# One of four channel tiles of a causal depthwise convolution computed on GpSimd

## The chip, the cores and the metric

The kernel runs on one core of a Trainium2 chip. A core has five engines that run their own queues of instructions side by side and meet at semaphores: TensorE (PE, matrix products), VectorE (DVE), ScalarE (ACT), GpSimd (POOL) and SyncE (SP, which here only issues DMAs). The metric is the time on the device of one execution in microseconds (us).

## What is computed

One transformer block (attention beside a gated linear recurrence, then an MLP) is followed by two layers of a second block. Both work on 256 tokens of width 2048 in float32. The change touches the second block alone, in each of whose layers a convolution runs over the tokens of 1024 channels, with a kernel of its own of 31 taps for every channel:

```python
u_val, u_gate = jnp.split(conv_in + glu_b[l], 2, axis=-1)
u = u_val * jax.nn.sigmoid(u_gate)
u = causal_depthwise_conv(u, dw_w[l], dw_b[l])        # 31 taps, groups = channels
u = jax.nn.silu(layer_norm(u, conv_ln_g[l], conv_ln_b[l]))
u = u @ w_pw[l] + b_pw[l]
conv_out = u * jax.nn.silu(conv_gate)
y = jnp.concatenate([mla_out, conv_out], axis=-1) @ w_out[l]
x = x + gate * y
```

## The kernel before

Every large product is made in three matmuls (or two wider ones) from a high and a low part of the weights and of the activations. Weights come by DMA into four buffers RAW0 to RAW3. A chunk is taken in halves: ScalarE copies a half into WH (line 1932), which rounds it, and VectorE subtracts that from RAW and writes the low part WL (line 1087). Such a subtraction is called a split here. There are four WH and four WL buffers (`NHL = 4`); ScalarE may write half j when TensorE has finished half j - 4 (`half_done`), VectorE when ScalarE has written it (`high`), and TensorE may use it when VectorE has split it (`split`). Nearly all of the kernel's time TensorE goes through one such half after another.

All smaller work is written as strands, generators that each engine's program steps once for every half of weights that TensorE takes. So on each engine a strand's piece stands in the queue between two halves, and its place is fixed when the program is built.

The convolution is such a strand. The channels are eight tiles of 128, four to a part. UV holds the gated input (256 tokens behind 30 zeros) and UG the running sum, both 128 x 256 for a tile. ScalarE makes tap 0 of each tile with the bias (line 2152), and VectorE adds taps 1 to 30 in place, one instruction a tap and tile (line 1446): 120 instructions for part 0 (tiles 0 to 3, semaphore `taps0`), 120 for part 1 (tiles 4 to 7, `taps1`). `tap_steps` orders them by tap, then tile, three or four in a step. Part 1 can start only when its gated input has been made, about halfway through. When both are done, `channel_norm` starts on TensorE with a sum over the channels (`n_sum`), ahead of which TensorE waits for `taps0` and `taps1`. GpSimd has nothing to do in this kernel.

Of the kernel before, what the change touches and what calls it, by code (L numbers as in the profile page):

```python
# [12 lines left out]
ALU = mybir.AluOpType  # L13
# [226 lines left out]
def weight_course(t):  # L240
# [105 lines left out]
    "ones_row lb lb_sig r_f r_log r_key r_cum r_last r_att r_diag r_gap r_exp0 r_edge r_cross r_ax "  # L346
    "r_diff r_exp r_pair r_level r_head r_out r_sq r_ss r_ms r_root r_wide r_unit r_done "
    "rope_v rope_t up_low up_sum up_relu up_sq up_h up_l "
    "gc uz taps0 taps1 l_sq l_ss l_rms l_root l_mul l_h l_l "
    "q_rope_sq h_sq h_sum h_rope_sum h_ms h_root h_gain h_rot h_sin h_rope h_wide h_apply "  # L350
    "a_score a_in a_top a_exp a_add a_probs a_tp a_pt a_pv a_out o_h o_l "
    "n_sum n_part n_mean n_sub n_sq n_ss n_ms n_root n_scale n_silu p_h p_l pw g_mm g_col g_out g_row g_mul x2"
# [3 lines left out]
def tiles(nc, ctx):  # L356

    ncol, nconst = columns()[1], constant_places()[1]
    m = {}

    def sb(c, name, shape, dt=F32, align=128):
        m[name] = c.enter_context(nc.sbuf_tensor(name, shape, dt, align_bytes=align))

    sb(ctx, "X", [128, 2, 2048], align=1024)
    sb(ctx, "HT", [128, 16, 2, 256], F32R)
    m["HTh"], m["HTl"] = m["HT"][:, :, 0, :], m["HT"][:, :, 1, :]
    for i in range(NRAW):
        sb(ctx, f"RAW{i}", [128, 2048])
    for i in range(NHL):
        sb(ctx, f"WH{i}", [128, 1024], F32R)  # L370
    for i in range(NHL):
        sb(ctx, f"WL{i}", [128, 1024], F32R)
    sb(ctx, "PK", [128, ncol])
    sb(ctx, "CN", [128, nconst])
    sb(ctx, "Y", [128, 2, 2048], align=1024)
    sb(ctx, "HS", [128, 256])
    with ExitStack() as c:
        for name in ("E1", "LK1"):
            sb(c, name, [128, 1024])
    sb(ctx, "CB", [128, 2048])  # L380
    sb(ctx, "ST", [128, 64])
    sb(ctx, "MODC", [128, 2, 3, 16])
    for i in range(8):
        m[f"PS{i}"] = ctx.enter_context(nc.psum_tensor(f"PS{i}", [128, 512], F32))
    sb(ctx, "VT", [128, 4, 256], align=1024)
    sb(ctx, "MXB", [128, 256])
    with ExitStack() as c:
        sb(c, "FR", [128, 8, 256])
        sb(c, "QR", [128, 8, 256])
        sb(c, "QA", [128, 8, 256])  # L390
        sb(c, "KA", [128, 256])
        sb(c, "VA", [128, 2, 128])
        sb(c, "SINK", [128, 16])
        sb(c, "S", [128, 8, 384])
        sb(c, "MX", [128, 4, 8])
        sb(c, "SM", [128, 2, 8])
        sb(c, "RES", [128, 1024])
        sb(c, "LB", [128, 2, 8])
        for name in ("LQ0", "LQ1"):
            sb(c, name, [128, 512])  # L400
        sb(c, "FC", [128, 16])
        sb(c, "AXX", [128, 2, 4, 128])
        with ExitStack() as d:
            for name in ("KK", "B", "E0", "LK0"):
                sb(d, name, [128, 1024])
        with ExitStack() as d:
            sb(d, "AH", [128, 8, 256], F32R, align=1024)
            sb(d, "AL", [128, 8, 256], F32R, align=1024)
    sb(ctx, "COS", [128, 256])
    sb(ctx, "SIN", [128, 256])  # L410
    with ExitStack() as c:
        sb(c, "GB1", [128, 2048])
        sb(c, "SJ", [128, 512])
    with ExitStack() as c:
        sb(c, "Uh", [128, 32, 256], F32R, align=1024)
        sb(c, "Ul", [128, 32, 256], F32R, align=1024)
    with ExitStack() as c:
        sb(c, "UV", [128, 8, 286])
        sb(c, "UG", [128, 8, 256])
        sb(c, "KV", [128, 3, 256])  # L420
        with ExitStack() as d:
            with ExitStack() as f:
                sb(f, "QN", [128, 8, 256], align=1024)
                sb(f, "QP", [128, 4, 256])
                sb(f, "KN", [128, 8, 256])
                sb(f, "KP", [128, 4, 256])
            with ExitStack() as f:
                sb(f, "GT", [128, 2048], align=1024)
                sb(f, "OH", [128, 8, 256], F32R, align=1024)
                sb(f, "OL", [128, 8, 256], F32R, align=1024)  # L430
            d.enter_context(nc.sbuf_tensor("SPACE", [128, 6144], F32, align_bytes=1024))
            sb(d, "V2", [128, 2, 1024])
            sb(d, "R2", [128, 256])
            with ExitStack() as f:
                sb(f, "KVh", [128, 2, 256], F32R, align=1024)
                sb(f, "KVl", [128, 2, 256], F32R)
                sb(f, "QLh", [128, 4, 256], F32R)
                sb(f, "QLl", [128, 4, 256], F32R)
            with ExitStack() as f:
                sb(f, "SQR", [128, 4, 256], align=1024)  # L440
            with ExitStack() as f:
                sb(f, "S2", [128, 8, 384], align=1024)
                sb(f, "MX2", [128, 2, 8])
                sb(f, "SM2", [128, 2, 8])
    return m


def views(m):

    col, place = columns()[0], constant_places()[0]  # L450

    def pk(name):
        a, n = col[name]
        return m["PK"][:, a:a + n]

    def cn(name):
        a, n = place[name]
        return m["CN"][:, a:a + n]

    return pk, cn  # L460
# [16 lines left out]
def tensor_program(e, m, signals, plan):  # L477
    chunks, group = plan
    pe = Queue(e, signals)
    pk, cn = views(m)  # L480
# [450 lines left out]
    def channel_norm(L, taps):  # L931
        UG, UV = m["UG"], m["UV"]
        while any(strand in course.strands for strand in taps):
            yield
        for n in range(15):
            if n == 0:
                b = small()
                pe.wait_ge("taps0", 124 * L + 124)
                pe.wait_ge("taps1", 124 * L + 124)
                spread_sum(b, lambda i: UG[:, i, :]).then_inc(signals["n_sum"], 1)  # L940
                free[b] = ("n_part", 2 * L + 1)
            if n == 2:
                b = small()
                pe.wait_ge("n_part", 2 * L + 1)
                mm(b, 0, 256, ones, m["R2"][:, :], True, True).then_inc(signals["n_sum"], 1)
                free[b] = ("n_mean", L + 1)
            if n == 6:
                b = small()
                spread_sum(b, lambda i: UV[:, i, 0:256], lambda i: ("n_sq", 4 * L + i // 2 + 1)).then_inc(
                    signals["n_ss"], 1)  # L950
                free[b] = ("n_part", 2 * L + 2)
            if n == 8:
                b = small()
                pe.wait_ge("n_part", 2 * L + 2)
                mm(b, 0, 256, ones, m["MXB"][:, :], True, True).then_inc(signals["n_ss"], 1)
                free[b] = ("n_root", L + 1)
            yield
# [61 lines left out]
    for L in range(2):  # L1019
# [10 lines left out]
        taps = [course.start(convolution(L, 0))]  # L1030
# [40 lines left out]
def vector_program(e, m, signals, plan):  # L1071
    chunks, group = plan
    dve = Queue(e, signals)
    pk, cn = views(m)
# [52 lines left out]
    def scaled(t, *cs):  # L1127
        for c in cs:
            e.tensor_scalar(Y[:, t, 512 * c:512 * c + 512], X[:, t, 512 * c:512 * c + 512], ST[:, 54 + t:55 + t], None,  # L1129
                            ALU.mult).then_inc(signals["xs"], 1)  # L1130
# [306 lines left out]
    def convolution(L, c0):  # L1437
        UV, UG = m["UV"], m["UG"]
        dw = pk(f"dw_w{L}").rearrange("p (c j) -> p c j", j=31)
        name = f"taps{c0 // 4}"  # L1440
        for turn_ in course.tap_steps(L, c0):
            for n in turn_:
                j, c = n // 4, c0 + n % 4
                if j:
                    dve.wait_ge(name, 124 * L + n - 3)
                    e.scalar_tensor_tensor(UG[:, c, :], UV[:, c, j:j + 256], dw[:, c, j:j + 1], UG[:, c, :], ALU.mult,  # L1446
                                           ALU.add).then_inc(signals[name], 1)
            yield
# [280 lines left out]
    for cg in range(3):  # L1729
        n = group["w_out", cg]  # L1730
# [3 lines left out]
    n = group["w_out", 3]  # L1734
# [27 lines left out]
    for half in range(2):  # L1762
        for g in range(16):
            n = group["w_up", 16 * half + g]
# [5 lines left out]
        for cg in range(4):  # L1770
            n = group["w_down", 4 * half + cg]
# [12 lines left out]
    for L in range(2):  # L1784
# [13 lines left out]
        UV, UG = m["UV"], m["UG"]  # L1798
# [116 lines left out]
                    row_rstd(54 + i)  # L1915
        if L == 0:
            scaled(1, 0, 1)


def scalar_program(e, m, signals, plan, t):  # L1920
# [788 lines left out]
def program(nc, t):  # L2709
    with ExitStack() as ctx:  # L2710
        m = tiles(nc, ctx)
        signals = {name: ctx.enter_context(nc.semaphore(name)) for name in SIGNALS}
        plan = weight_course(t)
        for layer in range(2):
            for n in ("w_in2", "w_q_up", "w_kv_up", "w_pw", "w_out2"):
                assert f"{n}_{layer}" in t
        with nc.Block() as block:
            block.tensor(lambda e: tensor_program(e, m, signals, plan))
            block.vector(lambda e: vector_program(e, m, signals, plan))
            block.scalar(lambda e: scalar_program(e, m, signals, plan, t))  # L2720
            block.sync(lambda e: sync_program(e, m, signals, plan, t))


# [109 lines left out]
```

## Time and profile before

| | |
|---|---|
| time, median of 3 runs | 1945.36 us (1945.29 to 1946.09) |
| the profiled execution | 1945.29 us, of which its span is 1943.5 us |
| TensorE busy | 1920.7 us (99%) |
| TensorE weight load | 1673.5 us (86%) |
| VectorE busy | 1527.1 us (79%) |
| ScalarE busy | 1068.5 us (55%) |
| GpSimd busy | 0.2 us (0%) |

The span runs from the first to the last instruction. A share of the span is an average over stages: in the stretches in which the convolution runs (about 1186 to 1400 us in layer 0, 1593 to 1805 us in layer 1) the engines stand otherwise than over the whole. A line number is that of the kernel before; helpers share a line (1083 is a tensor_tensor, whoever calls it), so tiles tell more than lines. L501 is any small matmul.

### The profile page before, as it was taken

The page shows a single profiled execution, that of the slowest core. Times are in us where ns is not written, and L with a number is a line of the kernel's source. Part 1 is how long each engine was busy: PE and PEld are TensorE (multiplying, and loading weights), DVE is VectorE, ACT ScalarE, POOL GpSimd, SP SyncE. Part 2 cuts the span into 40 slices and gives each one's busy share as a digit, 9 for nine tenths or more (in the row PEclk, how much of TensorE's full clock was granted, in tenths as well). Part 3 has the DMA queues.
Part 4 walks back from the last instruction along what each step waited for, and adds up shares of the span by engine and source line. Part 5 has one row for each costly group of instructions (what it writes and reads, how often), then busy time and mean ns, then how long its engine had stood idle before and what let it go on. Part 6 is the DMA issues. An engine that isn't in the chain of part 4 may idle for free.

```text
span 1943.5 us, 27681 instructions
## 1 busy us (share of the span) xinstructions
PE 1920.7 (99%) x11418; PEld 1673.5 (86%) x11418; DVE 1527.1 (79%) x2100; ACT 1068.5 (55%) x1549; POOL 0.2 (0%) x4
## 2 busy tenths in 40 slices
PE   7999999999999999999999999999999999999999
PEld 6888888888888888888888889999888898998897
DVE  6587776878888777888878578999966669999764
ACT  5575766455664443555544485554764656456742
POOL 0000000000000000000000000000000000000000
PEclk9999999999999999999999999999999999999999
DMA  7443445948899999989999634544455455454453
GB/s 284 154 162 123 148 152 185 365 145 300 328 340 340 343 339 339 335 323 341 330 337 358 243 131 155 203 164 141 152 195 190 140 191 174 152 174 136 171 196 126
DMA packets 63982, 442.58 MB, mean 228 GB/s; under 512 B 7249, under 2 KB 7537, under 8 KB 12401
## 3 DMA queue, kind: packets, MB, share of 16 engines
q1 hardware_dynamic: 61920, 434.30, 62.4%
q10 hardware_dynamic: 1936, 6.51, 1.0%
q8 instruction: 90, 1.47, 0.3%
q14 instruction: 36, 0.29, 0.0%
HBM read 438.67 MB, written 2.11 MB: 227 GB/s over the span
## 4 chain that ended last, share of the span: by engine, by line
PE 96%; DVE 2%; ACT 1%; DMA 0%; issue 0%; ACTq 0%; DVEq 0%
PE PS L630 24%; PE PS L634 12%; PE PS L509 11%; PE PS L511 11%; PE PS L510 11%; PE PS L578 6%; PE PS L501 6%; PE PS L579 6%; PE PS L580 6%; PE PS L659 1%; DMA X<-in_x 0%; DVE WL L1087 0%; ACT S L1995 0%; DVE Y L1129 0%; ACT WH L1932 0%
## 5 line engine op out<-in xcount | busy, mean ns | idle before, releaser
L1932 ACT ACTIVATE WH<-RAW 128x1024 fp32r<-128x1024 f32 (+1 forms) x636 | 662.8, 1048 | 726.2 <-PE PS L634 246.8
L1087 DVE TENSOR_TENSOR WL<-RAW,WH 128x1024 fp32r<-128x1024 f32 (+1 forms) x636 | 765.3, 1208 | 354.5 <-ACT WH L1932 353.3
L630 PE MATMUL PS<-HT,WH 128*128 128x512 f32 x2040 | 647.1, 398 | 0.0
L634 PEld LDWEIGHTS PS<-HT,WL 128*128 128x128 f32 x2040 | 383.2, 188 | 90.5
L634 PE MATMUL PS<-HT,WL 128*128 128x256 f32 x2040 | 401.3, 278 | 0.0
L630 PEld LDWEIGHTS PS<-HT,WH 128*128 128x128 f32 x2040 | 311.0, 189 | 7.7 <-issue 7.2
L578 PE MATMUL PS<-HT,WH 128*128 128x256 f32 x880 | 254.6, 289 | 1.4 <-DVE HT L1138 1.1
L580 PE MATMUL PS<-HT,WL 128*128 128x256 f32 x880 | 249.3, 283 | 0.0
L579 PE MATMUL PS<-HT,WH 128*128 128x256 f32 x880 | 249.3, 283 | 0.0
L1096 DVE SCALAR_TENSOR_TENSOR RAW<-RAW,CB 128x2048 f32<-128x2048 f32 x96 | 219.2, 2283 | 0.0
L1446 DVE SCALAR_TENSOR_TENSOR UG<-UV,PK,UG 128x256 f32<-128x256 f32 x480 | 200.0, 475 | 0.2
L509 PE MATMUL PS<-WH,Uh 128*128 128x512 f32 x512 | 199.2, 389 | 0.0
L510 PE MATMUL PS<-WL,Uh 128*128 128x512 f32 x512 | 199.2, 389 | 0.0
L511 PE MATMUL PS<-WH,Ul 128*128 128x512 f32 x512 | 199.2, 389 | 0.0
L578 PEld LDWEIGHTS PS<-HT,WH 128*128 128x128 f32 x880 | 169.0, 192 | 10.9 <-issue 7.8
L579 PEld LDWEIGHTS PS<-HT,WH 128*128 128x128 f32 x880 | 169.2, 192 | 0.3
L580 PEld LDWEIGHTS PS<-HT,WL 128*128 128x128 f32 x880 | 169.0, 192 | 0.0
L511 PEld LDWEIGHTS PS<-WH,Ul 128*128 128x128 f32 x512 | 96.1, 188 | 20.1
L510 PEld LDWEIGHTS PS<-WL,Uh 128*128 128x128 f32 x512 | 96.1, 188 | 19.8
L509 PEld LDWEIGHTS PS<-WH,Uh 128*128 128x128 f32 x512 | 96.1, 188 | 19.8
L509 PE MATMUL PS<-WH,HT 128*128 128x512 f32 x256 | 100.9, 394 | 0.0
L511 PE MATMUL PS<-WH,HT 128*128 128x512 f32 x256 | 99.8, 390 | 0.0
(319 smaller groups left out, 2025.1 us busy)
## 6 DMA issues: line engine op xcount, KB each, us to landing
RAW<-in_w_in SPq DMA_DIRECT2D x112, 1024.0 KB, 4.8
RAW<-in_ada_w SPq DMA_DIRECT2D x96, 1024.0 KB, 6.9
RAW<-in_w_up SPq DMA_DIRECT2D x64, 1024.0 KB, 6.9
RAW<-in_w_down SPq DMA_DIRECT2D x64, 1024.0 KB, 6.7
RAW<-in_w_out SPq DMA_DIRECT2D x48, 1024.0 KB, 4.9
RAW<-in_w_pw SPq DMA_DIRECT2D x8, 1024.0 KB, 4.9
RAW<-in_w_in SPq DMA_DIRECT2D x8, 768.0 KB, 4.2
RAW<-in_w_q_up SPq DMA_DIRECT2D x6, 1024.0 KB, 4.8
```

The source lines that it names most:

```text
L509: e.matmul(out, sh, mh, start=st, stop=False, skip_group_check=True)
L510: e.matmul(out, sh, ml, start=False, stop=False, skip_group_check=True)
L511: return e.matmul(out, sl, mh, start=False, stop=final, skip_group_check=True)
L578: e.matmul(out, sh, ah, start=first and i % 2 == 0, stop=False, skip_group_check=True)
L579: e.matmul(out, sh, al, start=False, stop=False, skip_group_check=True)
L580: op = e.matmul(out, sl, ah, start=False, stop=final, skip_group_check=True)
L630: e.matmul(bk[i][:, 0:512], wh[:, at], m["HT"][:, kt, :, :].rearrange("p a t -> p (a t)"), start=kt == 0, stop=False, skip_group_check=True)
L634: op = e.matmul(bk[i][:, 0:256], wl[:, at], HTh[:, kt, :], start=False, stop=kt == n.kts - 1, skip_group_check=True)
L1087: e.tensor_tensor(m[f"WL{j % NHL}"][:, 0:nk * w], m[f"RAW{i % NRAW}"][:, k0 * w:(k0 + nk) * w], m[f"WH{j % NHL}"][:, 0:nk * w].bitcast(F32 ...
L1096: e.scalar_tensor_tensor(raw[:, :], raw[:, :], 1.0, m["CB"][:, :], ALU.mult, ALU.mult, accum_out=mod[:, k:k + 1]).then_inc(signals["ada"], 1)
L1446: e.scalar_tensor_tensor(UG[:, c, :], UV[:, c, j:j + 256], dw[:, c, j:j + 1], UG[:, c, :], ALU.mult, ALU.add).then_inc(signals[name], 1)
L1932: e.activation(m[f"WH{j % NHL}"][:, 0:nk * w], m[f"RAW{i % NRAW}"][:, k0 * w:(k0 + nk) * w], ACT.Copy).then_inc(signals["high"], 1)
```

## The change

Tiles 3 and 7, the last of each part, leave VectorE. GpSimd makes each of their taps 1 to 30 in two instructions: a product of the shifted input with the tap's weight into a new tile PT1, and an addition of PT1 to the running sum. Each of the two waits for the one before it by a semaphore, `taps_p`. VectorE keeps the 90 instructions of the other three tiles in their steps; its wait for the tap before counts 3 back in place of 4. TensorE's `n_sum` waits for the 120 instructions of GpSimd too.

```diff
     sb(ctx, "VT", [128, 4, 256], align=1024)
+    sb(ctx, "PT1", [128, 256])
...
-                pe.wait_ge("taps0", 124 * L + 124)
-                pe.wait_ge("taps1", 124 * L + 124)
+                pe.wait_ge("taps0", 94 * L + 94)
+                pe.wait_ge("taps1", 94 * L + 94)
+                pe.wait_ge("taps_p", 120 * L + 120)
                 spread_sum(b, lambda i: UG[:, i, :]).then_inc(signals["n_sum"], 1)
...
                 j, c = n // 4, c0 + n % 4
-                if j:
-                    dve.wait_ge(name, 124 * L + n - 3)
+                if j and c % 4 < 3:
+                    dve.wait_ge(name, 94 * L + max(4, 3 * (j - 1) + c % 4 + 2))
                     e.scalar_tensor_tensor(UG[:, c, :], UV[:, c, j:j + 256], dw[:, c, j:j + 1], UG[:, c, :], ALU.mult,
                                            ALU.add).then_inc(signals[name], 1)
...
+def gpsimd_program(e, m, signals):
+    pool = Queue(e, signals)
+    pk = views(m)[0]
+    UV, UG = m["UV"], m["UG"]
+    done = 0
+    pool.wait_ge("pk", 16)
+    for L in range(2):
+        dw = pk(f"dw_w{L}").rearrange("p (c j) -> p c j", j=31)
+        for half, c in enumerate((3, 7)):
+            pool.wait_ge(f"taps{half}", 94 * L + 4)
+            for j in range(1, 31):
+                pool.wait_ge("taps_p", done)
+                e.tensor_scalar(m["PT1"][:, :], UV[:, c, j:j + 256], dw[:, c, j:j + 1], None, ALU.mult).then_inc(
+                    signals["taps_p"], 1)
+                pool.wait_ge("taps_p", done + 1)
+                e.tensor_tensor(UG[:, c, :], UG[:, c, :], m["PT1"][:, :], ALU.add).then_inc(signals["taps_p"], 1)
+                done += 2
...
+            block.gpsimd(lambda e: gpsimd_program(e, m, signals))
```

In VectorE's queue this is what stands near the end of part 0's first steps in layer 0, before the change. R is a reciprocal of the key latents, QN the query latents; WL<-RAW,WH is a split:

```order
L1446 SCALAR_TENSOR_TENSOR UG<-UV,PK,UG 128x256 x3
L1457 RECIPROCAL R<-R 128x256
L1087 TENSOR_TENSOR WL<-RAW,WH 128x1024
L1446 SCALAR_TENSOR_TENSOR UG<-UV,PK,UG 128x256 x3
L1461 SCALAR_TENSOR_TENSOR KV<-KV,PK,R 128x256 x2
L1087 TENSOR_TENSOR WL<-RAW,WH 128x1024
L1446 SCALAR_TENSOR_TENSOR UG<-UV,PK,UG 128x256 x3
L1087 TENSOR_TENSOR WL<-RAW,WH 128x1024
L1083 TENSOR_TENSOR QN<-PS,QN 128x256 x2
L1446 SCALAR_TENSOR_TENSOR UG<-UV,PK,UG 128x256 x3
```

And the same place after it, where the lines are two higher:

```order
L1448 SCALAR_TENSOR_TENSOR UG<-UV,PK,UG 128x256 x2
L1459 RECIPROCAL R<-R 128x256
L1089 TENSOR_TENSOR WL<-RAW,WH 128x1024
L1448 SCALAR_TENSOR_TENSOR UG<-UV,PK,UG 128x256 x2
L1463 SCALAR_TENSOR_TENSOR KV<-KV,PK,R 128x256 x2
L1089 TENSOR_TENSOR WL<-RAW,WH 128x1024
L1448 SCALAR_TENSOR_TENSOR UG<-UV,PK,UG 128x256 x2
L1089 TENSOR_TENSOR WL<-RAW,WH 128x1024
L1085 TENSOR_TENSOR QN<-PS,QN 128x256 x2
L1448 SCALAR_TENSOR_TENSOR UG<-UV,PK,UG 128x256 x3
```

The splits and all other work keep their places; a step has two or three taps where it had three or four.

GpSimd's queue is new. Here is the end of tile 3 and the start of tile 7 in layer 0, with the semaphores that each instruction waits for:

```order
L1934 TENSOR_SCALAR PT1<-UV,PK 128x256 [waits taps_p]
L1937 TENSOR_TENSOR UG<-UG,PT1 128x256 [waits taps_p]
L1934 TENSOR_SCALAR PT1<-UV,PK 128x256 [waits taps_p,taps1]
L1937 TENSOR_TENSOR UG<-UG,PT1 128x256 [waits taps_p]
L1934 TENSOR_SCALAR PT1<-UV,PK 128x256 [waits taps_p]
```

The third row is tile 7's first product: it stands behind all of tile 3 and waits for part 1's tap 0 as well.

TensorE's queue at `n_sum` after the change, in the middle of the products for the convolution's gates (PS2 and PS3 are accumulators in PSUM):

```order
L635 MATMUL PS<-HT,WL 128x256 x2
L502 MATMUL PS<-UG,CN 32x256 [waits taps_p,taps1,taps0]
L502 MATMUL PS<-UG,CN 32x256 x7
L631 MATMUL PS<-HT,WH 128x512 [waits split]
L631 MATMUL PS<-HT,WH 128x512
```

The sum stands where it stood; only its wait is longer, and the next half of weights is queued behind it.

## Rows read from the trace of the kernel before

**Rows 1.** The page's head: the span, and each engine's busy time, share, instructions.
```profile
span 1943.5 us, 27681 instructions
PE 1920.7 (99%) x11418; PEld 1673.5 (86%) x11418; DVE 1527.1 (79%) x2100; ACT 1068.5 (55%) x1549; POOL 0.2 (0%) x4
```

**Rows 2.** The chain that ended last: share of the span by engine.
```profile
PE 96%; DVE 2%; ACT 1%; DMA 0%; issue 0%; ACTq 0%; DVEq 0%
```

**Rows 3.** Busy time and instructions by stretch: the four parts of the convolution.
```profile
core 0: us, PE busy (x) PEld busy (x) DVE busy (x) ACT busy (x) POOL busy (x), PEclk, DMA share, GB/s
1186.00:1291.00 105.00, 105.00 (x778) 97.44 (x777) 103.26 (x186) 52.14 (x66) 0.00 (x0) 1.00 0.52 177
1291.00:1400.00 109.00, 109.00 (x803) 98.56 (x805) 108.34 (x216) 65.76 (x115) 0.00 (x0) 1.00 0.44 151
1593.00:1699.00 106.00, 106.00 (x787) 98.44 (x786) 104.26 (x188) 53.59 (x69) 0.00 (x0) 1.00 0.50 173
1699.00:1805.00 106.00, 106.00 (x779) 95.87 (x778) 105.34 (x210) 63.04 (x109) 0.00 (x0) 1.00 0.45 151
```

**Rows 4.** Waits of TensorE's weight load, 1186 to 1400 us: total us, times, longest.
```profile
PEld PS L578 <- issue: 3.3, 9, 0.4
PEld PS L501 <- issue: 2.6, 7, 0.4
PEld PS L578 <- DVE WL L1087: 0.7, 2, 0.4
```

**Rows 5.** VectorE's queue in order of time, 1296 to 1306 us: start, length.
```profile
1296.87 1.22 DVE L1087 TENSOR_TENSOR WL<-RAW,WH 128x1024 fp32r<-128x1024 f32 x1
1298.00 1.66 DVE L1446 SCALAR_TENSOR_TENSOR UG<-UV,PK,UG 128x256 f32<-128x256 f32 x4
1299.59 1.21 DVE L1087 TENSOR_TENSOR WL<-RAW,WH 128x1024 fp32r<-128x1024 f32 x1
1300.72 1.66 DVE L1446 SCALAR_TENSOR_TENSOR UG<-UV,PK,UG 128x256 f32<-128x256 f32 x4
```

**Rows 6.** VectorE's groups by form, 1186 to 1400 us: busy, mean ns, idle before.
```profile
L1446 DVE SCALAR_TENSOR_TENSOR UG<-UV,PK,UG 128x256 f32<-128x256 f32 x240 | 100.0, 475 | 0.1
L1087 DVE TENSOR_TENSOR WL<-RAW,WH 128x1024 fp32r<-128x1024 f32 x63 | 76.5, 1214 | 1.7 <-ACT WH L1932 1.6
L1476 DVE RECIPROCAL R<-R 128x256 f32<-128x256 f32 x1 | 1.7, 1742 | 0.0
L1083 DVE TENSOR_TENSOR QP<-QP,COS 128x1024 f32<-128x1024 f32 x1 | 1.2, 1205 | 0.0
L1502 DVE TENSOR_SCALAR QP<-QP,PK 128x1024 f32<-128x1024 f32 x1 | 0.7, 743 | 0.0
L1083 DVE TENSOR_TENSOR KV<-KV,COS 128x256 f32<-128x256 f32 x1 | 0.4, 416 | 0.0
L1502 DVE TENSOR_SCALAR KV<-KV,PK 128x256 f32<-128x256 f32 x1 | 0.3, 346 | 0.0
```

**Rows 7.** ScalarE's conversions by form, 1186 to 1400 us.
```profile
L1932 ACT ACTIVATE WH<-RAW 128x1024 fp32r<-128x1024 f32 x64 | 67.5, 1058 | 76.8 <-PE PS L580 59.4 <-PE PS L634 14.5 <-PE PS L511 2.8
```

**Rows 8.** Instructions on tile UG over both layers: ns min/median/max, first and last start.
```profile
L501 PE MATMUL PS<-UG,CN x32: 379/379/404, 1399.8 to 1807.0; 128*32 128x256 f32 x32
L2152 ACT ACTIVATE UG<-UV,PK x16: 587/594/603, 1181.9 to 1699.0; 128x256 f32<-128x256 f32 x16
```

**Rows 9.** ScalarE in order of time: tap 0 of part 1's four tiles.
```profile
1291.08 2.08 ACT L2152 ACTIVATE UG<-UV,PK 128x256 f32<-128x256 f32 x4 [3.77 <-DVE UV L1823]
```

**Rows 10.** Waits of TensorE over the span, the matmuls' and one of the weight load's.
```profile
PE PS L659 <- DVE Y L1129: 14.0, 3, 12.3
...
PEld PS L578 <- DVE WL L1087: 2.8, 5, 1.3
```

More of the change, by code:

```diff
@@ L348 @@
     "rope_v rope_t up_low up_sum up_relu up_sq up_h up_l "
-    "gc uz taps0 taps1 l_sq l_ss l_rms l_root l_mul l_h l_l "
+    "gc uz taps0 taps1 taps_p l_sq l_ss l_rms l_root l_mul l_h l_l "
     "q_rope_sq h_sq h_sum h_rope_sum h_ms h_root h_gain h_rot h_sin h_rope h_wide h_apply "
```

## The prediction

> **What bounds the kernel now.** I read the head of the page first. TensorE is busy for 1920.7 of 1943.5 us and VectorE for 1527.1 [rows 1], and the chain that ended last lies 96% on TensorE [rows 2]. A change on VectorE can shorten that chain only where TensorE waits for VectorE. Next come the stretches of the convolution, where the average deceives. The reader is to see two full columns: TensorE is busy throughout, and VectorE for 103.3 of 105 us, 108.3 of 109, 104.3 of 106 and 105.3 of 106 [rows 3]. Third, the waits: in layer 0's 214 us TensorE's weight load waited for a split 0.7 us in all [rows 4], and all waits for this line over the span make 2.8 us [rows 10]. VectorE keeps up with no margin, yet TensorE hardly waits. Last, ScalarE's conversions stood idle for 76.8 us with TensorE as the releaser [rows 7]: the weight buffers are mostly full, and TensorE sets the pace.
>
> How far VectorE may fall behind follows from the buffers. ScalarE can refill one when TensorE has freed it, and its turn comes three halves later. A half takes 2.72 us here, the distance of two splits (1296.87 and 1299.59) [rows 5], so 8.2 us. The conversion takes 1.06 [rows 7] and the split 1.21 [rows 5]; 5.9 us remain. That cushion is there at the start of part 0. At the start of part 1 I take it as empty, since VectorE is then at splits and taps without a gap [rows 5] and TensorE's weight load has just begun to wait for it [rows 4].
>
> **What leaves VectorE.** Four taps occupy it from 1298.00 to 1299.59 us, 0.40 each [rows 5] (475 ns is one's whole length [rows 6]; neighbours overlap). Thirty per tile are 12 us, 48 us for the four tiles. By itself this is worth at most what TensorE waits for splits in these stretches: 0.7 us in layer 0 and, the stages being alike, as much in layer 1, 1.4 us in all. The wait of three taps back costs nothing: three taps take 1.2 us and the one waited for is over after 0.48. The new tile PT1 only shifts addresses, at no cost, and the added semaphore wait of TensorE costs something only if GpSimd is late.
>
> **What GpSimd takes.** No row shows it at work on a tensor. For the length of its instructions I take the same operations at the same size on VectorE: the product is a TENSOR_SCALAR 128x256 with a scalar per partition, 346 ns, the addition a TENSOR_TENSOR 128x256 from SBUF, 416 ns [rows 6]; the mean is 0.38 us. The ends are 346 ns below, and above ScalarE's 594 ns, the slowest pass of this shape over a tile that uses the same scalars [rows 8]; 1742 ns for a RECIPROCAL [rows 6] is a repeated step for each element, which neither operation needs. At 0.38 the sixty instructions of a tile take 23 us; even at 1.7 us they would take 105, and part 1 leaves them 109 (1291 to the sum at 1399.8) [rows 8, 9]. So GpSimd alone is in time, with no other engine in its way.
>
> The Trainium skill has a figure (GPSIMD Engine Reference, Elementwise — side-by-side cycle accounting): about 2.6 cycles per element on GpSimd where VectorE needs one, so 256 elements at 1.2 GHz would be an estimate of 0.55 us for the addition. With that in place of 416 ns the mean would be 0.45 us and the sum below would give about 2025 us; no run here shows it yet.
>
> **What GpSimd takes from VectorE.** This is the disputed term, from nothing to the whole length of each of its 240 instructions. A row bears on it: VectorE passes 1024 columns in 743 ns with one tensor read (TENSOR_SCALAR) and in 1205 ns with two (TENSOR_TENSOR) [rows 6]. With one operand it goes almost twice as fast, so it has two ways to read, and an instruction with two operands from SBUF fills both. Splits and taps are of that kind, 176.5 of 211.6 busy us in layer 0 [rows 3, 6]. If GpSimd reads by one of these ways, a tap there (three operands read) stands in VectorE's way. I take the upper end: while a GpSimd instruction runs, VectorE stands still.
>
> The sum, for tile 3. After the removal VectorE has 103.3 - 12 = 91.3 us of work for 105 us of TensorE's, a load of 0.87, in 156 instructions of 0.585 us. GpSimd and VectorE alternate: each of the 60 turns takes 0.38 + 0.585, together 57.9 us, of which VectorE has 35.1. That feeds TensorE for 35.1/0.87 = 40.4 us. The deficit is 17.5 us, less the cushion 5.9: **11.6 us**. For tile 7: 96.3 us of work for 109 (0.883), 186 instructions of 0.518; 60 turns take 53.9 us, VectorE has 31.1, good for 35.2; deficit **18.7 us**. Layer 1 has nearly the same stretches [rows 3]. TensorE stands still for 2 x 30.3 = 60.6 us, and as it is the chain nothing later gives that back. From the profiled execution, 1943.5 + 1.8 outside = 1945.3 us, this makes 2005.9; the median of the runs is 0.1 higher: **2006 us**.
>
> With 594 ns the deficits are 30.3 - 5.9 = 24.4 and 31.5, twice that 112: 2057 us. With half of 0.38 us lost for VectorE in turns of the same length, tile 3 costs nothing (4.5 against the cushion of 5.9) and tile 7 5.8 us, in all 11.6: 1957 us. The point from which it costs: tile 7 breaks even at 0.10 us lost per GpSimd instruction, tile 3 at 0.21.
>
> **Rivals.** First, not slower: GpSimd reads by ways of its own. Then VectorE has 12 us of rest in each part, which nobody needs, since TensorE waited 1.4 us for splits and the sum keeps its place in the queue. For it speaks that no row shows a contention; against it the two rates above. Time 1944 to 1945 us. To be faster by over 0.2% the change would have to save 3.9 us, more than all waits of TensorE for splits.
>
> Second: both share, but VectorE keeps the way. Its neighbours overlap (four taps of 0.48 us in 1.66) [rows 5], so the next one may have claimed the reads before the last has ended; GpSimd then gets in only at a gap, about once between two splits. There are 65 steps of taps in a layer; at one instruction each, 65 of 120 are done when the sum is due, and 55 remain. TensorE waits for `taps_p` with all its queue behind it, VectorE runs dry, and GpSimd does them alone in 55 x 0.38 = 21 us, 42 for both layers: 1987 us. It decides below 1.85 instructions per step.
>
> On who yields, the Trainium skill states (SBUF — State Buffer, Who interferes with whom) that a VectorE instruction with two SBUF inputs contends with a GpSimd instruction that reads SBUF, and that the one that issued first holds the shared port for its whole length. By that rule the first rival falls and the time is that of the forecast or of the second, by order of issue. The rates of VectorE agree with two read ways; that one is shared no row here shows.
>
> **How the numbers follow.** Mutual blocking 0.58, VectorE keeps the way and GpSimd is late 0.15, no contention that matters 0.27 (0.04 of it faster by some saving that I don't see). The likeliest has its own range of 1957 to 2057 us. The whole range must hold part of the no-contention case too: 1943 to 2058. A measurement tells this kernel from no change at about 0.2%, 3.9 us: faster 0.04, within 0.23, slower 0.73.
>
> **What would show it.** Right: in the two stretches of each layer the means of taps (475 ns) and splits (1214 ns) grow while GpSimd is active and only then; TensorE's weight load waits tens of us for splits, ScalarE's conversions still for TensorE; GpSimd is done well ahead of the sum; the deficit is larger in part 1 than in part 0. Second rival: taps and splits keep their length, GpSimd's instructions are spread out or long, and TensorE waits at the sum for GpSimd. First rival: neither, and VectorE busy 12 us less in each stretch. The forecast is wrong in its size if GpSimd's instructions are not near 0.38 us, and in its kind if VectorE's lengths stay.

## The result and the profile after

The changed kernel takes 1970.7 us (1970.6 to 1971.2) against 1945.5 us for the kernel before: a ratio of 1.0131, 95% interval 1.0118 to 1.0143. It is slower, as forecast, but by 25 us where the forecast of 2006 us has 61: the sign was right, the size wrong.

The head of the page and the chain, of after, beside [rows 1, 2]:

```profile
span 1969.3 us, 27807 instructions
PE 1927.5 (98%) x11418; PEld 1678.2 (85%) x11418; DVE 1548.0 (79%) x1980; ACT 1067.1 (54%) x1549; POOL 287.0 (15%) x244
PE 80%; DVE 17%; ACT 2%; issue 1%; DMA 0%; ACTq 0%; DVEq 0%
```

The reader is to see an engine with less to do that is busy for longer: VectorE runs 120 instructions fewer (1980 for 2100) in 1548.0 us for 1527.1. It had 2% of the chain and has 17%. The same four stretches as [rows 3]:

```profile
core 0: us, PE busy (x) PEld busy (x) DVE busy (x) ACT busy (x) POOL busy (x), PEclk, DMA share, GB/s
1186.00:1291.00 105.00, 98.32 (x702) 90.01 (x701) 104.52 (x146) 49.57 (x64) 69.59 (x59) 0.98 0.47 161
1291.00:1400.00 109.00, 105.90 (x801) 96.74 (x800) 106.49 (x172) 59.13 (x95) 71.94 (x60) 1.00 0.44 151
1593.00:1699.00 106.00, 100.03 (x688) 90.68 (x687) 100.38 (x137) 52.12 (x71) 71.49 (x60) 0.97 0.48 166
1699.00:1805.00 106.00, 102.91 (x809) 95.89 (x808) 104.20 (x163) 53.13 (x76) 71.95 (x60) 1.00 0.43 148
```

In the first one 146 of VectorE's instructions lie where 186 lay; 30 of the 40 are the taps that left, so it is also behind by ten. TensorE's column is no longer full: 98.3 of 105 us. (Layer 1's stretches start some 12 us late here, so their borders cut elsewhere.) Where the lengths went, by VectorE's and GpSimd's groups by form, 1186 to 1412 us and whole span, beside [rows 6]:

```profile
L1448 DVE SCALAR_TENSOR_TENSOR UG<-UV,PK,UG 128x256 f32<-128x256 f32 x180 | 97.6, 594 | 0.1
L1089 DVE TENSOR_TENSOR WL<-RAW,WH 128x1024 fp32r<-128x1024 f32 x63 | 86.0, 1365 | 3.1 <-ACT WH L1953 3.0
...
L1934 POOL TENSOR_SCALAR PT<-UV,PK 128x256 f32<-128x256 f32 x120 | 183.4, 1528 | 1499.0 <-ACT UG L2173 1487.6
L1937 POOL TENSOR_TENSOR UG<-UG,PT 128x256 f32<-128x256 f32 x120 | 103.4, 862 | 10.0
```

The remaining 180 taps of layer 0 take nearly what 240 took (97.6 us, 100.0 before): 594 ns each for 475. What happens to one of them shows in order of time. First VectorE, then GpSimd, 1200 to 1206 us:

```profile
1200.38 1.76 DVE L1089 TENSOR_TENSOR WL<-RAW,WH 128x1024 fp32r<-128x1024 f32 x1
1202.07 1.09 DVE L1448 SCALAR_TENSOR_TENSOR UG<-UV,PK,UG 128x256 f32<-128x256 f32 x2
1203.08 1.75 DVE L1089 TENSOR_TENSOR WL<-RAW,WH 128x1024 fp32r<-128x1024 f32 x1
1204.75 1.09 DVE L1448 SCALAR_TENSOR_TENSOR UG<-UV,PK,UG 128x256 f32<-128x256 f32 x2
```

```profile
1200.32 0.74 POOL L1937 TENSOR_TENSOR UG<-UG,PT 128x256 f32<-128x256 f32 x1
1201.16 1.77 POOL L1934 TENSOR_SCALAR PT<-UV,PK 128x256 f32<-128x256 f32 x1
1203.02 0.72 POOL L1937 TENSOR_TENSOR UG<-UG,PT 128x256 f32<-128x256 f32 x1
1203.84 1.78 POOL L1934 TENSOR_SCALAR PT<-UV,PK 128x256 f32<-128x256 f32 x1
```

An addition starts at 1200.32; the split that starts 0.06 us later takes 1.76 us where it takes 1.21: it stood for 0.55 us. The product starts at 1201.16, in the middle of that split, and takes 1.77 us, though a product took 0.92 us at its shortest: it waited for the split's end. The pair of taps behind the split takes 1.09 us where two take 0.87 (0.40 and 0.48): 0.22 us lost, while the product read. So each engine holds the other off, and both were seen; that it is the reading that holds is for the experiments below. A pair of GpSimd's instructions takes 2.7 us here and costs VectorE 0.77.

Last, TensorE's waits in layer 0, 1186 to 1412 us (before, in about the same stretch, 0.7 us for splits and nothing for any other result [rows 4]):

```profile
PE PS L579 <- DVE KVl L1085: 2.8, 1, 2.8
PE PS L502 <- DVE HS L1522: 1.8, 2, 1.0
PE PS L502 <- DVE KV L1504: 1.7, 1, 1.7
PE PS L502 <- DVE QP L1533: 1.5, 1, 1.5
...
PEld PS L579 <- DVE WL L1089: 0.3, 1, 0.3
```

TensorE waits for VectorE, but hardly at the splits: at single small results of the latents (KVl, KV) and heads (HS, QP), once or twice each.

Not all of the 25 us is waiting. TensorE is busy for 6.8 us more than before (1927.5 for 1920.7) with the same 11418 matmuls, and its granted clock explains most of that. It was full in all four stretches before [rows 3]; here it fell three times to the lower of its two levels, 1.2 GHz, for some us:

```profile
core 0: us, PE busy (x) PEld busy (x) DVE busy (x) ACT busy (x) POOL busy (x), PEclk, DMA share, GB/s
1223.00:1229.00 6.00, 4.65 (x25) 4.47 (x25) 6.00 (x9) 0.07 (x1) 5.64 (x5) 0.72 0.72 265
1643.00:1649.00 6.00, 5.51 (x32) 5.25 (x33) 6.00 (x8) 0.99 (x2) 5.61 (x5) 0.72 0.76 258
1670.00:1676.00 6.00, 4.58 (x24) 4.43 (x25) 6.00 (x8) 0.82 (x2) 5.64 (x5) 0.72 0.40 135
```

The first time follows the wait for KVl, and a matmul then lasts 0.41 us where the same one lasts 0.28 at full clock:

```profile
1224.03 0.36 PE L579 MATMUL PS<-KVh,WH 128*128 128x256 f32 x1 [2.79 <-DVE KVl L1085]
1225.14 0.41 PE L579 MATMUL PS<-KVh,WH 128*128 128x256 f32 x1
1230.13 0.28 PE L579 MATMUL PS<-KVh,WH 128*128 128x256 f32 x1
```

A mean of 0.72 over 6 us is 1.7 us of full clock, so the three are worth at most 5.1 of the 25 us: VectorE catches up in the meantime, and a later wait may be shorter by as much.

### The profile page after: what moved, and what is told of

Read it like the earlier page. It is cut to its first block, busy times and chain, and to the rows that moved or that the text cites. A ratio compares the mean times of both kernels' runs of the same rounds, so it can differ in the third digit from the quotient of the medians.

```text
span 1969.3 us, 27807 instructions
## 1 busy us (share of the span) xinstructions
PE 1927.5 (98%) x11418; PEld 1678.2 (85%) x11418; DVE 1548.0 (79%) x1980; ACT 1067.1 (54%) x1549; POOL 287.0 (15%) x244
## 3 DMA queue, kind: packets, MB, share of 16 engines
q1 hardware_dynamic: 61920, 434.30, 61.7%
## 4 chain that ended last, share of the span: by engine, by line
PE 80%; DVE 17%; ACT 2%; issue 1%; DMA 0%; ACTq 0%; DVEq 0%
PE PS L631 22%; PE PS L635 11%; PE PS L510 11%; PE PS L512 11%; PE PS L511 11%; DVE UG L1448 6%; DVE WL L1089 6%; PE PS L502 4%; PE PS L579 3%; PE PS L581 3%; PE PS L580 3%; ACT WH L1953 1%; PE PS L660 1%; DMA X<-in_x 0%; DVE Y L1131 0%
## 5 line engine op out<-in xcount | busy, mean ns | idle before, releaser
L1089 DVE TENSOR_TENSOR WL<-RAW,WH 128x1024 fp32r<-128x1024 f32 (+1 forms) x636 | 788.1, 1243 | 359.3 <-ACT WH L1953 358.2
L1934 POOL TENSOR_SCALAR PT<-UV,PK 128x256 f32<-128x256 f32 x120 | 183.4, 1528 | 1499.0 <-ACT UG L2173 1487.6
L1448 DVE SCALAR_TENSOR_TENSOR UG<-UV,PK,UG 128x256 f32<-128x256 f32 x360 | 195.2, 594 | 0.2
L1937 POOL TENSOR_TENSOR UG<-UG,PT 128x256 f32<-128x256 f32 x120 | 103.4, 862 | 10.0
```

What stands on the lines that cost most here:

```text
L1089: e.tensor_tensor(m[f"WL{j % NHL}"][:, 0:nk * w], m[f"RAW{i % NRAW}"][:, k0 * w:(k0 + nk) * w], m[f"WH{j % NHL}"][:, 0:nk * w].bitcast(F32 ...
```

## The experiments

All ratios are to the kernel before. Where I say how late TensorE is at the end of a part, it is read from a mark in both traces: the end of part 0 where ScalarE stores the second gate group (UG<-PS), the end of part 1 at the first matmul of `n_sum`. What VectorE lost in a part is the sum, over all its instructions there, of length less the mean of the same instruction in the kernel before. For the changed kernel that makes 18.6 us in part 0 and 15.6 us in part 1 of layer 0.

### Relief without GpSimd

```diff
-            block.gpsimd(lambda e: gpsimd_program(e, m, signals))
```
The wait for `taps_p` goes too.

> Leaves out taps 1 to 30 of tiles 3 and 7 altogether: VectorE has the 90 taps per part of the changed kernel, GpSimd does nothing. Theory A (GpSimd's reads hold VectorE's instructions with two operands from SBUF; that alone costs): 1944 to 1946 us, taps at 475 ns again, VectorE 12 us less busy per part. Theory B (the cost comes from what else the change did: taps waiting three back, steps of two and three taps, the shifted addresses): some or all of the 25 us stay, 1955 to 1971 us.

1945.12 us, ratio 0.9999 (0.9990 to 1.0008); taps 478 ns. Theory A. The order of the taps, the wait of three back and the moved addresses cost nothing, and the relief is worth nothing. Its windows correct a term of the prediction:

```profile
1186.00:1291.00 105.00, 105.00 (x778) 97.47 (x777) 95.34 (x161) 55.10 (x71) 0.00 (x0) 1.00 0.51 177
1291.00:1400.00 109.00, 109.00 (x807) 98.56 (x809) 96.58 (x182) 63.01 (x110) 0.00 (x0) 1.00 0.45 155
```

With tile 3 gone VectorE has 95.3 us of work in part 0, not 91.3: in the kernel before it ended this stretch with some 4 us of its queue undone, so its busy time of 103.3 us was less than its work. The load is 0.908; in part 1 it is 0.886, as taken.

### Blocking without relief

```diff
-                e.tensor_tensor(UG[:, c, :], UG[:, c, :], m["PT1"][:, :], ALU.add).then_inc(signals["taps_p"], 1)
+                e.tensor_tensor(m["PT1"][:, :], m["PT1"][:, :], m["PT1"][:, :], ALU.add).then_inc(signals["taps_p"], 1)
```
VectorE's taps and the waits are those of the kernel before.

> All 240 taps per layer on VectorE as in the kernel before, and GpSimd makes its 120 products and 120 additions beside them, the additions on the spare tile PT1 (in place, both operands PT1) instead of the running sum. The blocking without the relief. Theory A: VectorE loses about 0.59 us per pair, 17.8 us per part, on a load of 0.98 to 0.99 where it had 12 us of room before: deficit about 17.8 less a cushion of up to 5.9 per part, 12 to 18 us, in all 48 to 71 us: 1993 to 2017 us. Theory B (the other parts of the change cost): they are taken back here, so 1945 to 1950 us. Under a theory that only small results are late by a fixed delay, about the 25 us of the changed kernel again: 1970 us.

1997.41 us, ratio 1.0269 (1.0253 to 1.0284): 52 us, in the range of theory A. VectorE lost 14.6 and 13.7 us in the parts of layer 0, and TensorE is 13.1 us late after part 0 and 25.7 after part 1. That is 25.7 of 28.3 us, but not all by waiting: over 1186 to 1306 and 1306 to 1425 us the granted clock was 0.97 and 0.96, worth up to some 8 us of the 25.7. The addition is not quite that of the change either. It reads one tile twice, lasts 0.61 us and holds a tap for 0.36 us, a split for 0.41.

### A stand-in for the lost time

```diff
+            if 0 < k < 27:
+                at = 26 * (2 * L + c0 // 4) + k
+                e.tensor_reduce(m["PT1"][:, at:at + 1], m["PK"][:, 0:512], AX.X, ALU.add)
```

> GpSimd does nothing and tiles 3 and 7 get no taps 1 to 30, as in relief; VectorE instead makes one idle pass per step in the first 26 steps of each part, a sum over 128x512 of a constant table into an unused column, about 0.67 us each: 17 us per part, placed where GpSimd was active. Theory A (the loss is VectorE's lost time in those 72 us, whatever takes it): within 6 us of the changed kernel, 1965 to 1977 us, with TensorE waiting at the same small results. If GpSimd hurts by something besides VectorE's time (memory of TensorE or ScalarE, semaphores): 1945 to 1955 us.

1956.07 us, ratio 1.0055 (1.0040 to 1.0070). Between the two expectations and only 1 us above the second, so neither number held. TensorE is 5.1 us late after part 0 and 5.2 after part 1, and its clock did not fall. The passes take 677 ns, with the overlap some 0.6, 15.6 us per part: 3 us less than GpSimd took in part 0; and in part 1 a step takes longer, so the 26 passes lie over 92 us (1297.7 to 1389.9) where GpSimd needed 77. A loss of VectorE's time alone does make TensorE late, without GpSimd, but by less than half of what the change costs, so by its time alone this run does not exclude that GpSimd also hurts in another way. Against that speak the lengths in the changed kernel, 1186 to 1412 us: ScalarE's conversions take 1057 ns (1058 before), TensorE's matmuls from HT 289 ns (289). And the formula used further down to account for the change gives these passes a cushion of 4.1 us in part 0, close to the 3.4 to 3.7 of the runs with GpSimd.

### The taps behind the small work

```diff
-            for n in turn_:
+            def taps(turn_=turn_):
+                for n in turn_:
...
+            course.late.append(taps)      # Course.beat runs these after all strands
```

> The changed kernel with one difference in VectorE's queue: in each step the taps stand behind the other strands' work of that step (latents, heads, attention) instead of ahead of it; nothing else moves. Theory C (TensorE waits for small results that stand behind delayed taps, a delay of one to two us each): a good part of the 25 us goes, 1950 to 1962 us. Theory D (VectorE's time as a whole is short by some 5 us per part, and order can't give it back): 1968 to 1973 us, with waits moved to the splits.

1968.92 us, ratio 1.0121 (1.0104 to 1.0138), 1.8 us less than the changed kernel. Theory D by its number; but the waits did not go to the splits. Waits of TensorE there, 1186 to 1412 us, are at other small results:

```profile
PE PS L583 <- DVE QN L1089: 3.1, 1, 3.1
PE PS L506 <- DVE HS L1528: 1.9, 2, 1.2
PE PS L506 <- DVE QP L1539: 1.5, 1, 1.5
PE PS L583 <- DVE KVl L1089: 0.9, 1, 0.9
```

The wait for KVl shrank from 2.8 to 0.9 us and one for QN came. Putting a result ahead moved the debt to the next: nearly all of it stayed.

### Products, additions and writes by themselves

GpSimd makes one kind of instruction, each waiting for the one before it; tiles 3 and 7 get no full sum.

```diff
-                e.tensor_tensor(UG[:, c, :], UG[:, c, :], m["PT1"][:, :], ALU.add).then_inc(signals["taps_p"], 1)
```

> GpSimd makes only the 120 products (into PT1, one waiting for the other), no additions; tiles 3 and 7 keep tap 0 alone. VectorE has 90 taps per part. Theory A (a GpSimd instruction holds a shared read way while it reads: 0.22 us for a product of 256 columns, one operand): blocked taps and splits are 0.22 us longer, never 0.54; VectorE loses at most 26 us in all, less than the 48 us of relief: 1944 to 1950 us. If both instructions hold equally (0.38 or more each): up to 46 us lost and lengths by 0.4 us: 1950 to 1958 us.

```diff
-                e.tensor_scalar(m["PT1"][:, :], UV[:, c, j:j + 256], dw[:, c, j:j + 1], None, ALU.mult).then_inc(
-                    signals["taps_p"], 1)
```

> GpSimd makes only the 120 additions (PT1, zeroed once, onto the running sum), no products. Theory A (two operands, 0.54 us of blocking each): taps and splits 0.54 us longer where hit; without the product between them the additions come every 0.9 to 1.6 us, so VectorE is slowed more per us but for a shorter time, 30 x 0.54 = 16 us per part against 12 freed: 1945 to 1962 us, more than products. If the product was the one that hurt: 1944 to 1947 us with lengths unchanged.

```diff
+            for j in range(60):
+                pool.wait_ge("taps_p", done)
+                e.memset(m["PT1"][:, :], 0.0).then_inc(signals["taps_p"], 1)
```

> GpSimd's 240 instructions are memsets of PT1 (128x256, one waiting for the other), which write and read nothing; tiles 3 and 7 keep tap 0 alone. Theory A (only reads are shared with VectorE's second operand): taps stay 475 ns and splits 1214, the time is that of relief, 1944 to 1946 us. If any GpSimd access holds VectorE: lengths grow by 0.2 us and more, up to 1950 us.

Taps on VectorE (layer 0) and GpSimd's own instructions, of products, additions and writes in this order:

```profile
L1448 DVE SCALAR_TENSOR_TENSOR UG<-UV,PK,UG 128x256 f32<-128x256 f32 x180 | 84.7, 522 | 0.1
L1934 POOL TENSOR_SCALAR PT<-UV,PK 128x256 f32<-128x256 f32 x120 | 167.3, 1394 | 1572.1 <-ACT UG L2171 1561.2
```

```profile
L1448 DVE SCALAR_TENSOR_TENSOR UG<-UV,PK,UG 128x256 f32<-128x256 f32 x180 | 96.4, 586 | 0.1
L1935 POOL TENSOR_TENSOR UG<-UG,PT 128x256 f32<-128x256 f32 x120 | 119.7, 998 | 1633.7 <-ACT UG L2171 1624.6
```

```profile
L1448 DVE SCALAR_TENSOR_TENSOR UG<-UV,PK,UG 128x256 f32<-128x256 f32 x180 | 76.4, 476 | 0.1
L1934 POOL MEMSET PT<- 128x256 f32 x240 | 75.8, 316 | 1642.8 <-ACT UG L2170 1629.2
```

Products: 1945.08 us (ratio 0.9999, 0.9990 to 1.0009); VectorE lost 9.4 us in layer 0, 0.16 per product. Writes: 1945.11 us (0.9999, 0.9990 to 1.0008); 240 instructions left the taps at 476 ns. Additions: 1979.26 us (1.0174, 1.0157 to 1.0191); VectorE lost 28.4 us in layer 0, 0.47 per addition. The order of the three is that of theory A, and what is shared is reading. But the additions' 34 us lie above every expectation, and above the changed kernel itself, though VectorE lost less than there (28.4 for 34.2 us). They come in 32 us per part (1184.1 to 1216.5 us in part 0) instead of 77: TensorE is 8.8 us late after part 0 and 17.1 after part 1. In part 0, where the clock stayed full, 14.1 us lost in 32 cost what 18.6 lost in 77 did: what a us costs depends on how many fall together. Part 1 has more to it. TensorE waited once for 6.1 us, for QP, and its granted clock was 0.66 over 1325 to 1335 us, worth up to 3.4 of the 8.3 us there.

What is held is not only what reads two tensors from SBUF. The pass over QP that TensorE waited for reads one tensor, at 743 ns [rows 6], and here it took 0.47 us longer in both layers. Passes that read PSUM, reductions and reciprocals kept their lengths beside GpSimd's additions. The first row is of additions, the second of the changed kernel, 1186 to 1412 us (414 ns before):

```profile
L1504 DVE TENSOR_SCALAR QP<-QP,PK x2: 1207/1208/1208, 1327.4 to 1751.0; 128x1024 f32<-128x1024 f32 x2
L1533 DVE TENSOR_TENSOR QP<-QP,PS 64x256 f32<-64x256 f32 x8 | 3.3, 415 | 0.1
```

### GpSimd spread over the part

```diff
+                pool.wait_ge(f"taps{half}", 94 * L + 4 + max(0, 3 * (j - 4)))
```

> The changed kernel with GpSimd's pairs paced: pair j may start only when VectorE has done tap j - 4 of its three tiles, so the 30 pairs of a part lie over the whole part (about 105 us) instead of its first 72. VectorE loses the same 17.8 us per part and is freed of 12 in the same span. If the loss is a local deficit (12 freed over 105 us, 17.8 lost in 72): the deficit falls to about 5 us per part against a cushion of 5.9: 1948 to 1960 us. If TensorE loses by the delay of single small results whenever GpSimd is active: 1968 to 1980 us, as more of them fall beside GpSimd's work.

1961.18 us, ratio 1.0081 (1.0066 to 1.0096), 9.5 us less than the changed kernel and 1.2 above the local deficit's range, some 7 below the other's. VectorE lost 15.5 and 13.4 us. TensorE is 5.4 us late after part 0 (9.0 in the changed kernel) and 7.9 after part 1 (12.5).

### One part alone, and the cushion

part0 and part1 give GpSimd one tile per layer; the other part is whole on VectorE (the edit shown is part1's). part1_eased is part1 with tile 3's taps left out. later is the changed kernel with a later start of tile 3, the second edit.

```diff
-        for half, c in enumerate((3, 7)):
+        for half, c in ((1, 7),):
```

> GpSimd takes tile 3 alone; part 1 is whole on VectorE (120 taps) as before. In the changed kernel TensorE was 9.0 us late at the end of part 0 in layer 0 and 12.5 us at the end of part 1. Theory E (a part costs its deficit of about 9.6 us less the cushion that VectorE has where GpSimd starts, about none early in part 0): 2 x 9.0 = 18 us, 1963 us. If both parts cost alike (half of 25 us each): 1958 us. If VectorE at full load in part 1 can't bring back what part 0 left late: above 1966 us.

> GpSimd takes tile 7 alone; part 0 is whole on VectorE (120 taps), so that VectorE comes to part 1 with no cushion, as in the kernel before and as the prediction took it. Theory E: the whole deficit of about 10 us per layer, against 3.5 us in the changed kernel: 1961 to 1966 us. If the cushion at the start doesn't matter: 2 x 3.5 = 7 us, 1952 us.

> As part1, but tile 3's taps 1 to 30 are left out altogether: VectorE has 90 taps in part 0 with no GpSimd beside them and comes to part 1 with its cushion. Theory E: 3.5 us per layer, 1950 to 1953 us, 10 us or more less than part1. If the cushion doesn't matter: the same as part1.

```diff
-            pool.wait_ge(f"taps{half}", 94 * L + 4)
+            pool.wait_ge(f"taps{half}", 94 * L + (31 if half == 0 else 4))
```

> The changed kernel, but GpSimd starts tile 3 only when VectorE has done nine taps of each of its three tiles, some 35 us later; nothing else moves. VectorE loses the same 18 us. Theory E (early in part 0 there is little cushion, later there are 6 us and more): part 0 costs 3 to 5 us in place of 9.0, with part 1 as it was or a little more: 1957 to 1962 us. If only the total of VectorE's time counts: 1970 us as before.

part0: 1963.71 us (1.0094, 1.0078 to 1.0111), as expected. part1_eased: 1952.59 us (1.0037, 1.0024 to 1.0050), as expected. part1: 1958.49 us (1.0067, 1.0052 to 1.0082), between its two numbers, 2.5 us below theory E's. later: 1970.33 us (1.0129, 1.0114 to 1.0144): a miss, the whole was not shorter. The marks of layer 0 say why. The gate group's store (ACT) is the end of part 0, of the kernel before, after and later in turn:

```profile
1264.33 1.57 ACT L2334 ACTIVATE UG<-PS,PK 128x256 f32<-128x256 f32 x4
```

```profile
1273.36 1.57 ACT L2355 ACTIVATE UG<-PS,PK 128x256 f32<-128x256 f32 x4
```

```profile
1269.98 1.57 ACT L2355 ACTIVATE UG<-PS,PK 128x256 f32<-128x256 f32 x4
```

And `n_sum`, first start in the last columns, of after, part1, part1_eased and later (1399.8 before [rows 8]):

```profile
L502 PE MATMUL PS<-UG,CN x32: 379/379/404, 1412.3 to 1832.8; 128*32 128x256 f32 x32
```

```profile
L502 PE MATMUL PS<-UG,CN x32: 379/379/404, 1406.3 to 1820.2; 128*32 128x256 f32 x32
```

```profile
L502 PE MATMUL PS<-UG,CN x32: 379/379/404, 1403.9 to 1814.6; 128*32 128x256 f32 x32
```

```profile
L502 PE MATMUL PS<-UG,CN x32: 379/379/404, 1412.1 to 1831.7; 128*32 128x256 f32 x32
```

Part 1 costs 6.5 us when VectorE comes to it full (part1) and 3.5 when it comes rested (12.5 - 9.0 in the changed kernel; 3.5 in part1_eased, which was 0.5 us late before its part 1). In later, part 0 did get cheaper, 5.7 us for 9.0, but GpSimd was then at tile 3 until 1289 us and left no time to recover: part 1 cost 12.3 - 5.7 = 6.6. The two differences cancel. The clock does not tell these apart: it fell once in part1's part 1 and not in later's, and they cost 6.5 and 6.6.

## Why the prediction was wrong

**The bound and the mechanism** were right. TensorE is the chain, the relief is worth nothing (relief: 0.9999), and GpSimd's reads hold VectorE's instructions with two operands from SBUF (products and additions do, writes don't). That was argued before from two rates; now it is shown, though the argument was too narrow: the faster of the two rates, with one operand, was held as well (additions: 1.21 us for 0.74). The Trainium skill states the contention (SBUF — State Buffer, Who interferes with whom), and the trace agrees in that the one that starts first holds the other off: products waited for splits as splits did for additions. It does not agree with the skill's hold for the whole instruction: a product of 0.92 us or more lengthened no tap or split of products by more than 0.23 us. The rival without contention is out. The rival in which GpSimd is late is out: it ended tile 7 at 1376.4 us, and the sum, due at 1399.8 before, began at 1412.3.

**The step that failed is the size of the two deficits**, 11.6 and 18.7 us, where 9.0 and 3.5 were measured. The forecast gave nothing to the clock; what it cost is inside the measured numbers. The formula holds up: of a stretch T in which VectorE loses L, TensorE is fed for (T - L)/load, and the rest less the cushion is the loss. Three of its inputs were off.

- The time lost. I took 0.38 us for each of 60 instructions, 22.8 us per part. The trace has 18.6 and 15.6. In the mean the blocks themselves are as large as taken (at most 0.55 and 0.23 us, mean 0.38), but not every instruction met one that it held, or held it in full: alone, an addition cost 0.47 us and a product 0.16. In part 1 this is worth 8 us of the 18.7, the largest single error.
- The length of a turn. A GpSimd instruction lasts longer than it holds: 0.92 us at least for a product that holds 0.22, 0.72 for an addition. Tile 3 took 76.8 us (1184.1 to 1260.9) and tile 7 77.3, not 57.9 and 53.9, and VectorE has the time between: by the forecast's own formula 3 us less of deficit in either part.
- The cushion. I gave part 0 5.9 us and part 1 none. Its load was taken 4 us too low as well (relief). With load 0.908 part 0 comes to 76.8 - 58.2/0.908 = 12.7 us, of which 9.0 arrived: a cushion of 3.7. The same sum gives 3.4 in later, 3.4 in additions and, for the passes of standin, 78.8 - 63.2/0.908 = 9.2 us, of which 5.1 arrived, 4.1. For part 1 the state at 1291 us was read from the kernel before, but the change itself takes it away: with 25% fewer taps and tile 3 done at 1261 us VectorE had time to recover before 1299. (Nor do [rows 4] show that TensorE had just begun to wait there: its two waits for a split lie between 1240 and 1285 us and after 1300.) The sum gives 77.3 - 61.7/0.886 = 7.7 us; 3.5 arrived, so a cushion of 4.2 (in standin 92.8 - 77.2/0.886 = 5.7 us, of which 0.1 arrived). Where it was empty, the whole deficit arrived: part1, 77.3 - 62.8/0.886 = 6.4 us and 6.5 measured; later 6.9 and 6.6. So the cushions are what is left over from the formula, not measured by themselves.

Two of the forecast's side sums are off, with no effect on it: sixty instructions of 1.7 us take 102 us, not 105, and with a mean of 0.45 us the sum gives 2023, not 2025.

**Where TensorE waits** was half wrong. I looked for tens of us at the splits; layer 0 has 0.7 us there and the rest at small results. Buffered weights don't help against a late KVl: TensorE waited 2.8 us for it. That this is why the cushion of part 0 is less than the 5.9 us of three buffered halves is an inference that no run tests. In additions, where the loss came densest, TensorE did wait 4.6 us for splits in part 0.

**GpSimd's durations.** My 346 and 416 ns (VectorE's rows) are neither the time that is held (0.22 and 0.55 us) nor the length of an instruction (0.92 and 0.72 us at least). Their mean of 0.38 us equals that of the two holds by luck: the product's is too large by about as much as the addition's is too small. The Trainium skill's 2.6 cycles per element (GPSIMD Engine Reference, Elementwise — side-by-side cycle accounting), an estimate of 0.55 us for the addition, agrees with the 0.55 us by which it held the split at 1200.38. Its whole reported length is 0.74 us, 0.2 more.

What stays open: the split of the cushion between splits and small results, and why spread, whose sum is 103.4 - 87.9/0.908 = 6.6 us for part 0, lost 5.4 of it, with hardly any cushion at work. The loads are means over a part, and the clock fell in this part too (0.72 over 1223 to 1229 us, up to 1.7 us); how much of the 5.4 is its own isn't separated. Nor is it for the changed kernel: layer 1's part 0, with two falls, cost 9.9 us where layer 0's, with one, cost 9.0.

No version here beats the kernel before. In relief and products VectorE had up to 24 us less work per layer and the time fell by 0.2 us, within the noise, so to take these taps off VectorE can't pay here.

## What to carry to other kernels

Before work is moved to GpSimd, ask how full VectorE is while it runs there, and how many of its instructions read two operands from SBUF: 12 us per tile were taken from VectorE and 13 to 19 given back as blocking (spread and the changed kernel). An engine that is 98% busy without holding anyone up gains nothing from relief and passes on what it loses beyond its cushion; dense losses cost more than spread ones (additions against spread). TensorE's granted clock can fall behind its waits, as it did here, so read it beside them. And read the cushion of a later stage as the change will leave it, not as the old kernel shows it.

## What the runs showed of the hardware

- A GpSimd addition of 128x256 float32 with two operands from SBUF lasts 0.72 to 0.74 us undisturbed. In additions it made a tap of VectorE up to 0.49 us longer and a split up to 0.55. A product with one operand lasts 0.92 us at least and made them at most 0.23 us longer (products).
- An addition also held VectorE's TENSOR_SCALAR of 128x1024 with one operand (1208 ns for 743, additions). VectorE's passes that read PSUM kept theirs (QP<-QP,PS 415 ns for 414, the changed kernel).
- Held by VectorE, the product takes up to 2.4 us (the changed kernel).
- GpSimd's writes (memset 128x256, 316 ns, 240 of them) left VectorE's taps unchanged (476 ns, 475 before).
- TensorE's granted clock fell to its lower level behind a wait of 2.8 us, and a matmul then took 0.41 us for 0.28 (the changed kernel, 1225 us).
